# First block of a two-block transformer on one core: modulation of a tile in one run, rank products two tiles behind, ten raw places

## The reference, cut to what matters

```
mod_in, modc_in = silu(c), silu(c_ctx)
sh1, sc1, gt1, sh2, sc2, gt2 = split(mod_in @ w_mod + b_mod, 6)      # and the same of modc_in
h  = rmsnorm(x,   g_attn) * (1 + sc1)  + sh1
hc = rmsnorm(ctx, g_attn) * (1 + csc1) + csh1
cq, ckv, kr, qn, kn, vn, f = split_columns(h @ w_in)                   # and the same of hc
...                                     # latent attention, neighbourhood attention, a Fourier mix, out, FFN
x = second_block(x)                     # window and stick-breaking attention, gates, FFN
```

## Time and profile before

| | |
|---|---|
| median of 3 runs | 2669.8 us (2667.35 to 2670.4) |
| profiled execution | 2670.11 us, its span 2668.3 us |
| PE busy | 2615.0 us (98%) |
| DVE, ACT, POOL busy | 1776.2, 1213.5, 32.4 us |
| chain that ended last | PE 95%, DVE 2%, ACT 1%, DMA 1% |
| DMA | 547.21 MB, 205 GB/s over the span |
| mean granted clock | 0.995 |

### The profile page before, as it was taken

How to read it: one execution, slowest core, us unless ns; L and a number is a source line. 1 busy time by engine, 2 the same in 40 slices (tenths; PEclk the granted TensorE clock), 3 DMA queues, 4 the chain that set the end, 5 groups by cost and what they waited for, 6 DMA issues and landing times.

```text
span 2668.3 us, 37181 instructions
## 1 busy us (share of the span) xinstructions
PE 2615.0 (98%) x15242; PEld 2235.9 (84%) x15242; DVE 1776.2 (67%) x2466; ACT 1213.5 (45%) x1595; POOL 32.4 (1%) x31
## 2 busy tenths in 40 slices
PE   6899999989999999999999999999999999999999
PEld 3568867878888888888888888899888888888888
DVE  3256886788888877555656667676866666665555
ACT  4342244445555555444533455455544444444443
POOL 2110000000000000000000000000000000000000
PEclk9999999999999999999999999999999999999999
DMA  8878884757777755555555534455565555556553
GB/s 321 299 266 285 285 289 159 243 181 235 241 231 242 231 190 191 189 190 190 185 188 189 182 135 142 143 183 189 179 199 190 190 191 188 191 188 192 191 190 122
DMA packets 151401, 547.21 MB, mean 205 GB/s; under 512 B 16960, under 2 KB 18880, under 8 KB 150464
## 3 DMA queue, kind: packets, MB, share of 16 engines
q1 hardware_dynamic: 148752, 540.35, 61.1%
q10 hardware_dynamic: 2480, 4.49, 0.6%
HBM read 542.68 MB, written 2.10 MB: 204 GB/s over the span
## 4 chain that ended last, share of the span: by engine, by line
PE 95%; DVE 2%; ACT 1%; DMA 1%; issue 0%; SPq 0%; POOL 0%; ACTq 0%; DVEq 0%
PE ps L453 46%; PE ps L452 24%; PE ps L457 3%; PE ps L458 3%; PE ps L459 3%; PE ps L450 3%; PE ps L465 2%; PE ps L463 2%; PE ps L464 2%; PE ps L451 1%; PE ps L1679 1%; DVE lo L405 1%; DMA raw<-in_stream 1%; PE ps L1890 1%; ACT hi L392 1%; PE ps L1862 1%
## 5 line engine op out<-in xcount | busy, mean ns | idle before, releaser
L405 DVE TENSOR_TENSOR lo<-raw,hi 128x1024 fp32r<-128x1024 f32 x822 | 1001.9, 1224 | 772.9 <-ACT hi L392 770.7
L453 PE MATMUL ps<-pair,hi 128*128 128x512 f32 x3994 | 1391.8, 392 | 0.0
L392 ACT ACTIVATE hi<-raw 128x1024 fp32r<-128x1024 f32 x822 | 867.9, 1059 | 1093.3 <-PE ps L453 908.6
L452 PE MATMUL ps<-pair,lo 128*128 128x256 f32 x3994 | 1120.1, 280 | 0.0
L453 PEld LDWEIGHTS ps<-pair,hi 128*128 128x128 f32 x3994 | 750.5, 188 | 161.5
L452 PEld LDWEIGHTS ps<-pair,lo 128*128 128x128 f32 x3994 | 750.6, 188 | 6.0 <-issue 2.4
L453 PE MATMUL ps<-hid,hi 128*128 128x512 f32 x1376 | 477.4, 392 | 0.0
L452 PE MATMUL ps<-hid,lo 128*128 128x256 f32 x1376 | 384.6, 280 | 0.0
L453 PEld LDWEIGHTS ps<-hid,hi 128*128 128x128 f32 x1376 | 258.3, 188 | 56.7
L452 PEld LDWEIGHTS ps<-hid,lo 128*128 128x128 f32 x1376 | 258.3, 188 | 0.3
L1276 DVE TENSOR_REDUCE tmp<-ps 128x256 f32<-128x512 f32 x260 | 176.4, 683 | 5.0 <-PE ps L453 4.6
(11 more groups left out here) (316 smaller groups left out, 2297.0 us busy)
## 6 DMA issues: line engine op xcount, KB each, us to landing
raw<-in_stream SPq DMA_DIRECT2D x1014, 512.0 KB, 4.2
xc<-in_xc SPq DMA_DIRECT2D x4, 1024.0 KB, 8.7
x<-in_x ACTq DMA_DIRECT2D x1, 2048.0 KB, 7.6
out<-out_sb SPq DMA_DIRECT2D x8, 256.0 KB, 2.8
c_bc<-in_c_bc SPq DMA_DIRECT2D x1, 1024.0 KB, 7.8
bias<-in_rpb ACTq DMA_DIRECT2D x4, 256.0 KB, 4.5
raw<-in_stream SPq DMA_DIRECT2D x2, 256.0 KB, 3.4
dft<-in_dft_tab ACTq DMA_DIRECT2D x1, 512.0 KB, 6.0
```

Source lines behind the costliest of these rows:

```text
L392: e.activation(hi[:, c % R, :], raw_of(p), ACT.Copy).then_inc(hi_ready, 1)
L405: e.tensor_tensor(lo[:, c % R, :], raw_of(p), hi[:, c % R, :].bitcast(F32), ALU.subtract)\
L452: e.matmul(out[:, T:2 * T], wlo, act[:, 0, :], start=False, stop=False)
L453: return e.matmul(out, whi, both_, start=False, stop=last)
```

## The change

1. PE's loop of the front does the four `modulate` of tile kt in a row, then all eight output tiles of `first(kt - 2)`, then `turn_mod(kt)` (not of kt - 1). `turn_mod(0)` stands before the loop. ACT copies the row of tile kt first, then splits chunk kt - 1 and does `first_hi(kt - 1)`; DVE does `split_lo` and `first_lo` of kt - 1 and then `modulation(kt)`.
2. In the stream the weights of tile kt - 1 stand behind the four mod chunks of tile kt.
3. Up to the last rank chunk the stream uses ten places: the six of `raw` and four in `raw_deep`, in space that `ckvn` takes afterwards. PLACE, NTH and PREV take over what p % RR and p // RR said. From there on it is six places again.
4. No extras stand at `kr` 1 and `kn` 0 and 1; `vn` 1 to 4 have three instead of two, and one more stands in `out`. The silu of `c_bc` moves from the loop to behind the three copies of the rotary key, and the table of the square root is loaded again right behind it.
5. The copies of `f_sb` move from step 8 to the end of step 7.
6. Some semaphores are merged (`cvec` with `base`, `c_bc` with `rope`, the tables of the second block; `csil_zeroed` with `zeroed`).

```diff
+DEEP = 4
-EXTRA = {AT[("kr", 1)]: 1}
+EXTRA = {}
...
+    for _i in range(2 if _s == "kn" else 0, sum(q[0] == _s for q in CHUNKS)):
+        EXTRA[AT[(_s, _i)]] = _per + (_s == "vn" and 1 <= _i <= 4)
...
 for _kt in range(KT):
-    SEQ.append(("mod", 4 * _kt))
-    if LAG <= _kt:
-        SEQ.append(("weights", _kt - LAG))
-    SEQ.extend(("mod", 4 * _kt + _i) for _i in range(1, 4))
+    SEQ.extend(("mod", 4 * _kt + _i) for _i in range(4))
+    if LAG - 1 <= _kt:
+        SEQ.append(("weights", _kt - LAG + 1))
...
+N_DEEP = POS[("weights", AT[("a", KT - 1)])] + 1
+PLACE = [_p % (RR + DEEP) if _p < N_DEEP else (_p - N_DEEP) % RR for _p in range(len(SEQ))]
+for _p, _at in enumerate(PLACE):
+    PREV.append(_held[_at][0] if _at in _held else None)
+    NTH.append(_held[_at][1] + 1 if _at in _held else 1)
+    _held[_at] = (_p, NTH[-1])
...
+        raw_deep, _ = place("raw_deep", [P, DEEP, CH], at=reg + 64 * K1)
...
             def load(p):
-                if p >= RR:
-                    kind, i = SEQ[p - RR]
+                if PREV[p] is not None:
+                    kind, i = SEQ[PREV[p]]
...  ACT
+            rows(0)
...
-            for kt in range(KT):
-                if kt >= LAG:
-                    split_hi(e, kt - LAG, kt - LAG + 1)
-                if kt:
-                    first_hi(kt - 1)
+            for kt in range(1, KT):
                 rows(kt)
-                if kt == 11:
-                    e.wait_ge(s_cbc, 16)
-                    e.activation(c_bc[:], c_bc[:], ACT.Silu).then_inc(c_ready, 1)
+                if kt >= LAG - 1:
+                    split_hi(e, kt - LAG + 1, kt - LAG + 2)
+                    first_hi(kt - LAG + 1)
...
             e.activation(kro[64:P, 1, :], ps[64:P, 6, T:2 * T], ACT.Copy).then_inc(kr_copied, 1)
+            e.wait_ge(s_cbc_rope, 32)
+            e.activation(c_bc[:], c_bc[:], ACT.Silu).then_inc(c_ready, 1)
+            e.preload_act_table_set("sqrt_and_others")
...
-                    if n == CPG:
-                        e.wait_ge(weights_used, BASE["f"] + CPG)
-                        for tt in range(2):
-                            e.activation(f_sb[:, tt, :], ps[:, 1 + tt, :], ACT.Copy).then_inc(f_copied, 1)
...
+                if n == CPG - 1:
+                    e.wait_ge(weights_used, BASE["f"] + CPG)
+                    for tt in range(2):
+                        e.activation(f_sb[:, tt, :], ps[:, 1 + tt, :], ACT.Copy).then_inc(f_copied, 1)
...  DVE
+            for kt in range(KT):
+                if kt >= LAG - 1:
+                    split_lo(e, kt - LAG + 1, kt - LAG + 2)
+                    first_lo(kt - LAG + 1)
+                modulation(kt)
...  PE
+            turn_mod(0)
             for kt in range(1, KT):
                 for i in range(4):
                     modulate(kt, i)
-                    if i == 0:
-                        turn_mod(kt - 1)
-                    if kt >= LAG:
-                        first(kt - LAG, ((0, 1, 4), (2, 3), (5, 6), (7,))[i])
-            turn_mod(KT - 1)
-            first(KT - 2)
+                if kt >= LAG:
+                    first(kt - LAG)
+                turn_mod(kt)
+            for kt in range(KT - LAG, KT - 1):
+                first(kt)
             rotary(0)
```

More of the change, by code:

```diff
@@ L100 @@
 for _kt in range(KT):
-    SEQ.append(("mod", 4 * _kt))
-    if LAG <= _kt:
-        SEQ.append(("weights", _kt - LAG))
-    SEQ.extend(("mod", 4 * _kt + _i) for _i in range(1, 4))
-for _c in range(KT - LAG, N_CHUNKS):
+    SEQ.extend(("mod", 4 * _kt + _i) for _i in range(4))
+    if LAG - 1 <= _kt:
+        SEQ.append(("weights", _kt - LAG + 1))
+for _c in range(KT - LAG + 1, N_CHUNKS):
     SEQ.append(("weights", _c))
@@ L374, in raw_of @@
         def raw_of(p):
-            return raw[:, p % RR, :]
+            return raw[:, PLACE[p], :] if PLACE[p] < RR else raw_deep[:, PLACE[p] - RR, :]
         def split_view(part, c, k, n):
@@ L382, in split_hi @@
                 p = POS[("weights", c)]
-                e.wait_ge(landed[p % RR], 16 * (p // RR + 1))
+                e.wait_ge(landed[PLACE[p]], 16 * NTH[p])
                 if c >= R:
@@ L500, in load @@
                 if SEQ[p][0] == "weights" and CHUNKS[SEQ[p][1]][0] == "kr":
-                    e.dma_start(raw_of(p)[:, 0:CH // 2], stream[p, :, 0:CH // 2]).then_inc(landed[p % RR], 16)
+                    e.dma_start(raw_of(p)[:, 0:CH // 2], stream[p, :, 0:CH // 2]).then_inc(landed[PLACE[p]], 16)
                 else:
-                    e.dma_start(raw_of(p), stream[p]).then_inc(landed[p % RR], 16)
+                    e.dma_start(raw_of(p), stream[p]).then_inc(landed[PLACE[p]], 16)
             for i in range(4):
@@ L708, in _ @@
                 .then_inc(stdx, 1)
-            for kt in range(KT):
-                if kt >= LAG:
-                    split_hi(e, kt - LAG, kt - LAG + 1)
-                if kt:
-                    first_hi(kt - 1)
-                rows(kt)
-                if kt == 11:
-                    e.wait_ge(s_cbc, 16)
-                    e.activation(c_bc[:], c_bc[:], ACT.Silu).then_inc(c_ready, 1)
-            split_hi(e, KT - LAG, KT - LAG + 1)
-            first_hi(KT - 1)
-            at = KT - LAG + 1
+            for kt in range(1, KT):
+                rows(kt)
+                if kt >= LAG - 1:
+                    split_hi(e, kt - LAG + 1, kt - LAG + 2)
+                    first_hi(kt - LAG + 1)
+            for kt in range(KT - LAG + 1, KT):
+                split_hi(e, kt, kt + 1)
+                first_hi(kt)
+            at = KT
             to = BASE["kn"] + 2
@@ L1133, in _ @@
             e.wait_ge(s_vecs, 16)
-            for kt in range(1, KT):
-                if kt >= LAG:
[L1136 to L1142, removed]
+            for kt in range(KT):
[3 more added lines that the diff above has]
+                modulation(kt)
+            for kt in range(KT - LAG + 1, KT):
+                split_lo(e, kt, kt + 1)
+                first_lo(kt)
+            at = KT
             to = BASE["kn"] + 2
@@ L1698, in in_x, with first @@
                              kt == KT - 1)
-            def first(kt, tiles=range(8)):
+            def first(kt):
                 c = AT[("a", kt)]
-                if tiles[0] == 0:
-                    e.wait_ge(lo_ready, c + 1)
-                    e.wait_ge(xc_lo, kt + 1)
+                e.wait_ge(lo_ready, c + 1)
+                e.wait_ge(xc_lo, kt + 1)
                 whi, wlo = hi[:, c % R], lo[:, c % R]
-                for m in tiles:
+                for m in range(8):
                     w = slice(m * P, (m + 1) * P)
@@ L1711, in first @@
                         r = in_both(kt, m - 2, whi[:, w], wlo[:, w])
-                if tiles[-1] == 7:
-                    r.then_inc(weights_used, 1)
+                r.then_inc(weights_used, 1)
             def rotary(i):
```

48 lines of the change are left out of this document (23 added, 25 removed).

## The result

The changed kernel takes **2628.14 us** (median of 4 runs, 2628.07 to 2628.91), the kernel before on the same chip 2670.1 (4 runs): a ratio of 0.985 with an interval of [0.9838, 0.9862]. It is 42 us faster; 2630 was forecast, in a range of 2624 to 2646. The profiled execution took 2628.91 us, its span is 2627.1 (2668.3 before), so 41.2 us of span have to be found.

The account below looks back on a forecast made before the run. PE was taken to bound the front through switching and waits for split weights; start 2.3, loop 27.4, tail 5.5 and `f_sb` 4.2 sum to 39.4 us off 2670.11, giving 2630 us, range 2624 to 2646.

Parts of the forecast that it names:

- What bounds the kernel: Front loop: PE's switching and its wait for split weights set the 8.60 us tile period, not the stream.
- The new period: Front loop: mod chunks 1.71, output tiles 4.21, one switch pair 0.34 and the turn make 6.86 us a tile.
- The dearer price of four chunks in a row: Front loop: upper price of four mod chunks at full clock, 2.28 us instead of 1.71, adding 0.57 a tile.
- Do waits replace it: Front loop: ACT and DVE finish the splits and first products 2.8 us before PE wants them.
- The stream: Front loads: at 415 GB/s a tile needs 6.3 us, so the stream stays hidden with 4 us to spare.
- One of the forecast's own signs of being wrong: Front loop: the forecast is wrong if mod chunks wait for the stream after tile 3.
- The start and the tail: Before tile 3 and from tile 15 to `kn`: 2.3 us and 5.5 us gained.
- The silu beside `kn`: At `kn`: silu and table loads cost ACT 4.5 us, hidden with 2.1 us of cover before PE wants `kn` 2.
- The extras: Dots moved away from `kr` and `kn`, a third added at `vn` 1 to 4: zero effect.
- `f_sb`: Steps 7 and 8: moving the copies removes PE's 2.85 us wait and 1.4 us at low clock, 4.2 us.

Follow-up runs that it names:

- `e_before_ten`: The kernel before with only the ten stream places and the merged semaphores added; 2669.26 us, ratio 1.0002.
- `e_silu_loop`: The changed kernel with the silu of `c_bc` back in the loop at kt = 11 and no table load beside `kn`; 2628.66 us.
- `e_light_pe`: The changed kernel without output tiles 6 and 7 of `first` for feature tiles 1 to 13, all transfers kept; 2626.46 us.
- `e_f_back`: The changed kernel with the two copies of `f_sb` back in step 8; 2632.54 us.
- `e_switch`: The changed kernel with one narrow output tile behind each of the first three mod chunks, the other five behind the fourth; 2642.08 us.

## Why the prediction was right, step by step

- **What bounds the kernel.** Right: PE in the front, by switches and by the wait at the turn. `e_before_ten` shows that the stream wasn't it.
- **The new period**, 6.86 us. The parts were right, two terms a little large: the turn with the way into it takes 0.43 us instead of 0.6, and the chunks with their switch 1.97 instead of 2.05 (61.37 + 0.11 - 59.51, the first output matmul taking 0.11 more than its 0.117); the output tiles take 4.23 against 4.21. The dearer price of four chunks in a row (2.28 us) did not show. 12 x 0.23 us, less the stop of 1.1, is why the loop gave 29.0 instead of 27.4.
- **Do waits replace it.** Right: no wait for `both` or `lo` stands in the loop; the 2.8 us of cover took even a silu of 3.2 us with a single wait of 0.5 (`e_silu_loop`).
- **The stream.** Right in the outcome, wrong in the margin. 415 GB/s from seven microseconds was read as the rate of eighty; it is 408. With PE faster than forecast too, 4 us of slack became one stop of 1.1 us, and 0.2 us a tile remain (`e_light_pe`). One of the forecast's own signs of being wrong, a mod chunk that waits for the stream after tile 3, did show, once (88.43). That it stayed at one stop is in part luck: a stream slower by 4% would have set the period. The page "DMA: Bandwidth & Descriptors" of the Trainium skill, section "Where 436 GB/s comes from", gets its 358 GB/s as half of what a stack of memory gives to two cores. With one core at work the trace here does not agree, it shows 408.
- **The start and the tail**, 2.3 and 5.6 us, where 2.3 and 5.5 were forecast. The tail is as worked out: 26.3 us from the start of tile 15 (120.28) to `kn`, against 26.4. That the start agrees to the tenth is luck. `first(0)` began 0.4 us later than forecast and lost 0.4 less to the low clock, and in `e_f_back`, with the same work up to there, turn 2 stands 2.3 us earlier.
- **The silu beside `kn`.** As worked out to a few tenths. ACT in the changed kernel, in order of time:

```profile
148.87 1.28 ACT L761 ACT_TABLE_LOAD   x1
150.16 1.92 ACT L761 ACTIVATE c_bc<-c_bc 128x2048 f32<-128x2048 f32 x1
152.10 1.28 ACT L762 ACT_TABLE_LOAD   x1
153.40 2.01 ACT L403 ACTIVATE hi<-raw 128x1024 fp32r<-128x1024 f32 x2
```

  Both activations follow their load by 1.29 to 1.30 us, so the drain that "ScalarE: Activation LUTs" of the Trainium skill, section "What ACT_TABLE_LOAD costs", adds to make 2.66 us isn't seen here. The remainder of `kn` 2 is done at about 155.7, PE wants it at 157.9: 2.2 us of cover, where 2.1 were forecast.
- **The extras**: zero is right against the kernel before, but for a reason that was only half of it. I had counted three dots that leave this place, and there are five (one at `kr` 1, two each at `kn` 0 and 1). And I had looked at the cover of the split of `kn` 2, not at the norms of the rank products behind the same dots, whose PSUM `kn` takes over: left where they were, the dots would have brought a new wait, 1.4 us in all.
- **`f_sb`**: 4.2 forecast, 4.4 in the trace, 4.3 and 4.1 in the two runs that move it alone.

The sum was 39.4 us, the span gave 41.2; of the 1.8 between them 1.6 are the loop. What stays open is why the start differs from profile to profile. Turn 2 stands between 36.87 and 39.19 us in kernels whose work ahead of it is the same. A part is the first load, for which PE's first matmul waits until 15.43 us (`e_silu_loop`) to 16.33 (changed kernel). Another is where the clock rises: in `e_f_back` `first(0)` has the full clock from its start at 32.54, in the changed kernel it starts at 33.44 and its narrow output tiles still run at the low one. Why it rises earlier in the one than in the other, no run tells.

## What to carry to other kernels

Where PE shows as busy, take the interval of a repeated piece apart into its matmuls' own pace: what is left over is switching, and it can be had by grouping alike matmuls. Grouping on one engine must go together with the order on the engines that feed it: whoever hands over a result only at the end of a group must not stand, on the reader's queue, ahead of work for the next group. More places for a stream were worth nothing while its consumer took 8.6 us a tile, and 7 to 8 us in all once it was nearly as fast as the stream, at 6.6 against 6.4. At that point take them, and take every transfer that isn't wanted yet out of that stretch. A still faster consumer gains next to nothing there (`e_light_pe`).

## What the runs showed of the hardware

- A change on PE between the fp32 mod chunks (four quarters of the array side by side) and the output tiles on the whole array, there and back, costs 0.33 to 0.34 us at the full clock, all of it shown as busy (`e_switch`).
- One core's loads, nearly all of 512 KB to 1 MB, ran at 403 to 424 GB/s from 5 to 120 us without a dip (changed kernel, 5 us a figure).
- A table load on ACT takes 1.28 us, and the next activation starts 1.29 to 1.30 us after the load has started (148.87 and 150.16, 152.10 and 153.40).
